# Gate and up weights of the experts loaded as pairs of rows a partition, and token rows transposed with a column step of two

## The reference, cut to what matters

```python
logits = t @ w_router + b_router                 # 16 experts in 4 groups
probs  = softmax(logits)                         # best group, then its best two experts, weights renormalised
h = silu(einsum('nd,edf->nef', t, w_gate)) * einsum('nd,edf->nef', t, w_up)
h = h * gate[:, :, None]                         # zero but for the two chosen experts
moe = einsum('nef,efd->nd', h, w_down)
x = layernorm(ALPHA * x + moe)
```

## Time and profile before

| | |
|---|---|
| median of three runs | 1697.02 us (1696.25 to 1697.19) |
| profiled execution, span from first to last instruction | 1697.9 us; the profile gives this execution no other time |
| expert stage, first load to last instruction | about 1312 to 1698 us |
| its tiles on TensorE, first transpose to last matmul | 1337.1 to 1656 us |
| TensorE busy over the span | 1596.4 us (94%) |

### The profile page before, as it was taken

One profiled execution on the slowest core, in us unless ns is written; L12 is line 12 of the kernel. 1 busy time (PEld: TensorE's weight loads), 2 busy tenths in 40 slices (PEclk: granted clock), 3 DMA queues, 4 the chain that ended last, 5 costly groups with the idle time before them and its releaser, 6 DMA issues. The chain is left out here.

```text
span 1697.9 us, 25703 instructions
## 1 busy us (share of the span) xinstructions
PE 1596.4 (94%) x9847; PEld 1467.2 (86%) x9847; DVE 819.4 (48%) x1362; ACT 663.2 (39%) x1117; POOL 238.6 (14%) x292
## 2 busy tenths in 40 slices
PE   7999999999999999999999999999997599999980
PEld 7999898889988898999999999999786488888870
DVE  4433463453033433322042223234647799999975
ACT  5422241221245544421112111112212488888866
POOL 1000120013011111130000000000000244543320
PEclk9999999999999999999999999999998699999995
DMA  6111232124211112062325214112432899999746
GB/s 183 41 38 39 77 115 52 27 77 155 78 48 59 52 43 80 19 206 64 124 73 170 63 50 143 38 38 83 161 119 92 271 270 277 324 287 289 196 66 229
DMA packets 154225, 204.34 MB, mean 120 GB/s; under 512 B 14723, under 2 KB 121235, under 8 KB 154104
## 3 DMA queue, kind: packets, MB, share of 16 engines
q1 hardware_dynamic: 135224, 140.82, 26.5%
q0 software_dynamic: 18880, 61.89, 13.1%
HBM read 152.34 MB, written 50.34 MB: 119 GB/s over the span
## 5 line engine op out<-in xcount | busy, mean ns | idle before, releaser
L380 PE MATMUL ps<-xh,slab_hi 128*128 128x384 f32 (+1 forms) x504 | 170.3, 338 | 1.3 <-DVE slab_lo L733 1.3
L380 PE MATMUL ps<-xh,slab_lo 128*128 128x384 f32 (+1 forms) x504 | 165.2, 328 | 0.0
L380 PE MATMUL ps<-xl,slab_hi 128*128 128x384 f32 (+1 forms) x504 | 165.0, 327 | 0.0
L1901 PE MATMUL ps<-xh,slab_lo 128*128 128x384 f32 (+1 forms) x384 | 125.2, 326 | 0.0
L1901 PE MATMUL ps<-xh,slab_hi 128*128 128x384 f32 (+1 forms) x384 | 125.1, 326 | 0.0
L1901 PE MATMUL ps<-xl,slab_hi 128*128 128x384 f32 (+1 forms) x384 | 125.1, 326 | 0.0
L2102 DVE TENSOR_TENSOR gt_sg<-ps,gt_sg 128x384 f32<-128x384 f32 (+1 forms) x48 | 25.7, 536 | 186.4 <-PE ps L1901 186.2
L380 PEld LDWEIGHTS ps<-xh,slab_hi 128*128 128x128 f32 x504 | 95.1, 189 | 11.5 <-issue 9.7
L2871 PE MATMUL ps<-mo_hi_gu,mo_xh 128*128 128x512 f32 x256 | 100.3, 397 | 0.9 <-ACT mo_xh L2974 0.7
L2871 PE MATMUL ps<-mo_hi_gu,mo_xl 128*128 128x512 f32 x256 | 99.1, 392 | 0.0
L2042 ACT ACTIVATE gt_sg<-ps 128x384 f32<-128x384 f32 (+1 forms) x48 | 22.8, 474 | 190.9 <-PE ps L1901 190.9
(11 more groups left out here) (500 smaller groups left out, 4225.8 us busy)
## 6 DMA issues: line engine op xcount, KB each, us to landing
slab_raw<-in_w_in SPq DMA_DIRECT2D x60, 512.0 KB, 4.3
mo_raw_g<-in_w_e_gate SPq DMA_DIRECT2D x16, 1024.0 KB
mo_raw_u<-in_w_e_up SPq DMA_DIRECT2D x16, 1024.0 KB
mo_raw_d<-in_w_e_down SPq DMA_DIRECT2D x16, 1024.0 KB
gt_oh<-oT_hi SPq DMA_DIRECT2D x3, 2176.0 KB, 7.9
gt_ol<-oT_lo SPq DMA_DIRECT2D x3, 2176.0 KB, 12.7
slab_raw<-in_w_branch SPq DMA_DIRECT2D x24, 256.0 KB, 4.7
x_dram<-slab_raw SPq DMA_DIRECT2D x9, 512.0 KB, 5.1
```

Source lines behind the costliest of these rows:

```text
L380: mm = eng.matmul(out, w[:, b, k, :], x[:, k, t0:t0 + tn], start=(k == 0 and j == 0), stop=(k == KC - 1 and j == 2), skip_group_check=True)
L1901: last = eng.matmul(out, w[:, s % 2, c, wk, :], x[:, k, t0:t0 + tn], start=(k == 0 and i == 0), stop=(k == ks[-1] and i == 2))
```

## The change

The destination of the gate and up loads is unchanged in bytes. The source now gives partition p two neighbouring rows of every 256: block 2k + j of partition p holds row 256k + 2p + j. The two rows are neighbours in memory, so that a run is 2 KB, and there are four a partition. The transposes follow: piece 2k + j takes columns 256k + j, 256k + j + 2, ... of the token rows, 128 columns at a step of two numbers (8 bytes). All that comes after reads the same tiles with the same patterns.

```diff
             def load_gu(x):
                 for buf, w in ((raw_g, sh.w_e_gate), (raw_u, sh.w_e_up)):
-                    eng.dma_start(buf[:, x % RGU, :].rearrange("p (k n) -> p k n", k=KC),
-                                  w[0, x].rearrange("(k p) n -> p k n", p=128)).then_inc(gu_in[x % RGU], 16)
+                    eng.dma_start(buf[:, x % RGU, :].rearrange("p (k n) -> p k n", k=KC // 2),
+                                  w[0, x].rearrange("(k p j) n -> p k (j n)", p=128, j=2)).then_inc(gu_in[x % RGU], 16)
...
                 for half in range(2):
                     for k in range(4):
-                        c0 = 128 * (4 * half + k)
-                        last = eng.transpose(sh.ps[:, half, 128 * k:128 * k + 128], xg[:, i % RX, c0:c0 + 128], sh.ident[:, :])
+                        c0 = 256 * (2 * half + k // 2)
+                        last = eng.transpose(sh.ps[:, half, 128 * k:128 * k + 128], xg[:, i % RX, c0 + k % 2:c0 + 256:2],
+                                             sh.ident[:, :])
                     last.then_inc(x_tr, 1)
```

## The result

The changed kernel takes 1703.01 us (median of 9 runs, 1699.24 to 1706.54); the kernel before, run beside it, 1697.02 (9 runs, 1694.83 to 1699.89). The ratio is 1.0035, with a 95% interval of 1.0026 to 1.0045: slower by 6.0 us, where I had forecast 1696.0 and no change. The time lies 2.6 us above the 1700.4 at which I had called the forecast wrong, and 0.3 us above the upper end of the wide range, 1702.7. The profiled execution took 1706.0 us, 3 us more than the median; its span is 1704.4 us, against 1697.9 before. So the two profiles lie somewhat further apart than the medians.

What follows compares the result with a forecast made beforehand. The prediction took TensorE to bound the expert stage, loads hidden. From the median 1697.02 us it took 1 us for the add chain and zero for transposes and the rest: 1696.0, "no change"; own range 1693.6 to 1699, wide range 1690.5 to 1702.7.

Steps and rivals of the forecast that it cites:

- What bounds the kernel: Expert stage: TensorE binds at 9.31 us a tile, VectorE just behind, and TensorE never waits for a DMA.
- The loads: Gate and up loads: 16384 fewer packets, 386 GB/s, about 9.1 us less DMA time, hidden behind TensorE's tile.
- the three hundredths forecast: Sign in the profile after: the DMA share from 1400 to 1500 us should fall by three hundredths.
- The 1 us for the add chain: y copy's 1.1 us wait for GpSimd's adds: lighter DMA load lets the chain keep up; 1 us off, bounds 0 and 2.1.
- The other wait, for a landing: ScalarE's one wait for a landing that SyncE reports, 1.0 us in the kernel before; no time taken off for it.
- The price by packet: DMA cost taken as 37.9 ns a KB plus 8.9 ns a packet, assumed from 1 KB and 4 KB runs.
- The transposes: 256 transposes on TensorE reading columns 8 bytes apart: price zero, by the rank counts' row; upper bound 36.6 us.
- Rival 3: Slower: the transposes' stepped weight load has a price; a tenth gives 1700.7 us, double 1733; chance 0.12.
- My rival's smallest case: Transposes on TensorE: only a tenth of 143 ns more a weight load, 3.7 us in all, 1700.7 us.
- Rival 1: Faster: the expert stage's small waits are DMA contention, and relief gives back 5.7 us, 1691.3; chance 0.21.
- Rival 2: Slower: larger weight packets delay GpSimd's adds in the DMA engines, 5.7 us more, 1702.7; chance 0.07.
- Rival 4: Gate and up loads don't become faster with 2 KB runs; time stays 1697.0 us; chance 0.10.

Runs made afterwards that it cites:

- extra1: Kernel before with one block of each tile transposed twice, contiguously, old loads: 1.0032 of the kernel before.
- early_before: Kernel before with VectorE's and ScalarE's register reads issued earlier, ahead of their waits: 0.9942 of the kernel before, 0.9952 in the second series.
- steps_only: Kernel before with only the stepped transposes, loads left in 1 KB runs (pairing wrong): 1.0018 of the kernel before.
- early_after: Changed kernel with VectorE's and ScalarE's register reads issued earlier: 0.9970 of the kernel before, 0.9973 in the second series.
- beside_after: Changed kernel with each stepped transpose put behind one of the eight tail matmuls in place of eight in a row: 1.0031 of the kernel before.
- step4: The change carried to four neighbouring rows a partition, 4 KB runs and columns 16 bytes apart: 1.0032 of the kernel before.
- loads_only: Kernel before with only the 2 KB loads, transposes left contiguous (pairing wrong): 1.0011 of the kernel before, 1.0007 when run again.
- step8: The change carried to eight neighbouring rows a partition, 8 KB runs and columns 32 bytes apart: 1.0040 of the kernel before.
- early_loads4: Kernel before with gate and up loads in 4 KB runs, contiguous transposes (pairing wrong) and early register reads: 0.9957 of the kernel before.
- early_act: Kernel before with only ScalarE's register reads issued earlier, ahead of the y copies: 0.9953 of the kernel before.
- early_dve: Kernel before with only VectorE's register read issued earlier: 0.9987 of the kernel before.
- early_loads: Kernel before with 2 KB loads, contiguous transposes (pairing wrong) and early register reads: 0.9953 of the kernel before, 0.9947 in the second series.

## Why the prediction was wrong

**What bounds the kernel.** Right: TensorE. `extra1` shows it, and `early_before` shows 100.00 us busy of 100 (99.0 in the earlier trace rows).

**The loads.** Packets, 388 GB/s for 386 and the hiding were right. The DMA share fell by twice the three hundredths forecast, but by four hundredths with the old loads too (0.98 in `steps_only`): a stretch with less work in it, and so luck in part. The 1 us for the add chain was wrong. Its wait went and no time came back, since TensorE, not ScalarE, ends the tile; and it went in `steps_only` too, so the relief of the DMA engines was not the reason. The other wait, for a landing, grew from 1.0 to 3.7 us where I had left it at 1.0. The price by packet, drawn from 1 and 4 KB runs, held for 2 KB. The Trainium skill (DMA: Bandwidth & Descriptors, "Why small descriptors are slow (HBM only)") gives 4% from 1 to 2 KB by its beats, as worked out in the prediction; 350 to 388 GB/s is 11%, so the rows are right and the rule too small here.

**The transposes: the step that failed.** "I take zero, by that row." This term of the sum is the mis-sized one: for zero, the step by itself costs 3.1 us in `steps_only` and 3.6 to 4.7 with early reads. The row was the nearest by its step, but it showed the operand that streams through the array, at half the clock, in another type. The operand that changed is the one that is loaded into it, and there the step costs 69 ns of 140. Rival 3 named this mechanism with a chance of 0.12. Of the bounds, 0 to 36.6 us, I had called the upper one all on the path, yet the chain of `early_after` shows that of 256 x 0.069 = 17.7 us of longer loads 32 x 0.09 = 2.9 us are on it (by the plain tiles of before and after, 32 x 0.11 = 3.5). My rival's smallest case, a tenth of a load all on the path (3.7 us), came near this by two errors that cancel: the price is half a load, and a sixth to a fifth of it shows.

The Trainium skill (SBUF — State Buffer, the note on "cachelines") says that two hits on a 16-byte line keep full rate, and puts the stride that is free at 4 elements of fp32. For this weight load it doesn't hold: 209 ns with two hits a line, 210 at a step of 4 elements, and less, 192 ns, at a step of 8.

**The feedback.** I treated the other waits as fixed. In the two profiles the direct term is 3.2 to 3.5 us of 6.3, and 3.0 lie in longer slow tiles and the last tile. TensorE's wait for gate and up tails, 5.0 us before, is 8.1, 6.5 in `steps_only`, 6.7 in `extra1`, 6.9 in `beside_after` and 8.0 in `step4`, all with a longer tile on TensorE, and 4.9 in `loads_only`, with the old one. Only `step8`, whose tile is 0.04 us longer, stays at 4.9; there the wait for the hidden row's tail has grown, from 1.6 to 2.3. Without slow tiles the change costs 3.6 to 4.7 us, with them 6.0 (4.4 to 7.6). The intervals overlap, so that the feedback is a cost of its own of 1 to 2 us is likely by the traces and not settled by the times. Nor is the sum of the halves, 3.1 + 1.2 or 1.9, different from 6.0 by more than the runs vary.

**The rivals.** Rival 1 fell: idle time rose from 7.2 to 9.1 us. It was right that these waits were worth several microseconds, but lighter loads don't give them back and earlier register reads do. Whether full DMA engines have a part in how long such a read takes, no run tells. Rival 2 fell by its own sign: the eight adds that were 9.93 us apart are 9.56 apart in the changed kernel (lines below), and 9.62 in `steps_only`; and larger runs still, `early_loads4`, leave the tile at 9.31. Rival 4 fell with 388 GB/s.

```profile
1507.90 1.59 POOL L2825 DMA_INDIRECT acc_dram<-mo_y,mo_slot_idx  x1 [6.58 <-DMA acc_dram<-mo_y,mo_slot_idx]
...
1584.41 1.58 POOL L2825 DMA_INDIRECT acc_dram<-mo_y,mo_slot_idx  x1 [6.50 <-DMA acc_dram<-mo_y,mo_slot_idx]
```

**What stays open:** how a stepped load comes to 209 ns and why it is less at 32 bytes; whether the loads cost 1 to 2 us in the kernel with slow tiles; why a register read at times takes several times as long; what let the clock fall back in one tile of two kernels; and what in `step8` takes back the 0.07 us a tile that it saves.

The best version is `early_before`, the kernel before with its register reads moved: 1688.2 and 1688.5 us in its two series, 0.5% under the kernel before. `early_act`, with ScalarE's reads alone, can't be told from it (1688.9). The change adds nothing to it.

## What to carry to other kernels

Before a layout is changed to make loads faster, ask whose time it takes on the other side: here 9 us of hidden DMA time were bought with 3 us of the engine that binds. Price an operand only by a row of the same role (loaded or streamed) and type; without one, let the forecast and the range lean to the dear side. And where three engines pass work around near their limit, look in the chain for time marked "issue" between a wait's end and the instruction behind it: reading registers ahead of the wait took it away. Don't rank such gaps by length: here the shorter one, which stood in plain tiles too, was worth nearly all of the gain, and the longer one, which came only with the slow tiles, 2 of some 9 us. Moving each alone told them apart.

## What the hardware showed

- A 128 x 128 fp32 weight load takes 140 ns from contiguous columns, 209, 210 and 192 ns at steps of 8, 16 and 32 bytes. Eight transposes in a row hold TensorE for 0.87 us, or 0.95 at 8 bytes.
- Loads alone on the DMA engines: 350 GB/s in 1 KB runs, 388 in 2 KB, 406 to 408 in 4 KB.
- A transpose with the 8-byte step behind each 512-column matmul takes 0.12 us, no less than in a row.
- ScalarE's two register reads hold it for 0.6 us in most tiles, and at times longer: 1.7 us once in `early_dve`, 2.1 us once in the kernel before (ahead of 1507.92).
- With TensorE's granted clock at 0.84 and 0.74 over two stretches of 4 us, one tile took 13.1 us in place of 11.5 (`early_loads`, `early_before`).
